# A gated recurrence on one core: decay exponents of all levels formed by VectorE, scaled inside the exponential

## The reference, cut to what matters

```
gla_log_a = log_sigmoid(glr_up) / 16
bcum  = cumsum(log_g)                        # within a chunk
decay = exp(bcum[i] - bcum[j])  for j <= i
scores[i, j] = sum_d q[i, d] k[j, d] decay[i, j, d]
o_intra = scores @ v
chunk_kv = (k * exp(b_last - bcum))^T @ v
S = exp(b_last) * S_before + chunk_kv
o_inter = (q * exp(bcum)) @ S_before
```

## Time and profile before

| what | value |
|---|---|
| time, median of 3 runs | 2365.45 us (2363.62 to 2366.69) |
| the profiled execution's own time | 2366.69 us |
| its span in the profile | 2364.9 us |
| PE busy | 2317.5 us, 98% of the span |
| DVE busy | 1290.9 us, 55% |
| ACT busy | 953.8 us, 40% |
| POOL busy | 793.8 us, 34% |
| mean granted PE clock | 0.996 of full speed |

### The profile page before, as it was taken

The page is one execution under the profiler, slowest core; times in us unless marked ns, Lnnn a source line. Parts: engine busy times, 40 slices in busy tenths (PEclk is TensorE's granted clock), DMA queues, the critical chain, the costliest instruction groups (busy, mean ns, idle before and its releaser), DMA issues.

```text
span 2364.9 us, 37976 instructions
## 1 busy us (share of the span) xinstructions
PE 2317.5 (98%) x14904; PEld 2017.3 (85%) x14904; DVE 1290.9 (55%) x2607; ACT 953.8 (40%) x1890; POOL 793.8 (34%) x707
## 2 busy tenths in 40 slices
PE   8999999999999999999999999999999999999998
PEld 7889978898888899887888898888899888888898
DVE  4003268889987433471333556456456456578746
ACT  5124665555554432332222333343343334455320
POOL 3121325555563221414442333233233242232112
PEclk9999999999999999999999999999999999999999
DMA  6234334343334421232334424324314314475621
GB/s 257 88 126 162 136 138 149 128 147 113 119 137 177 158 99 63 98 116 93 110 118 132 160 72 152 116 72 152 116 68 152 116 72 184 143 271 178 231 90 72
DMA packets 137004, 312.20 MB, mean 132 GB/s; under 512 B 12288, under 2 KB 51840, under 8 KB 125568
## 3 DMA queue, kind: packets, MB, share of 16 engines
q1 hardware_dynamic: 80192, 223.85, 27.7%
q10 hardware_dynamic: 56640, 86.00, 9.9%
HBM read 211.77 MB, written 98.04 MB: 131 GB/s over the span
## 4 chain that ended last, share of the span: by engine, by line
PE 92%; DVE 4%; DMA 1%; ACT 1%; issue 1%; POOL 0%; ACTq 0%; DVEq 0%; POOLq 0%; SPq 0%
PE bank L415 13%; PE bank L417 13%; PE bank L416 13%; PE bank L426 6%; PE bank L427 6%; PE bank L428 6%; PE bank L2702 3%; PE bank L2679 3%; PE bank L2020 3%; PE bank L2021 3%; PE bank L2022 3%; PE bank L1599 2%; PE bank L507 2%; PE bank L508 2%; PE bank L509 2%; PE bank L2668 1%
## 5 line engine op out<-in xcount | busy, mean ns | idle before, releaser
L415 PE MATMUL bank<-at_hi,w_hi 128*128 128x512 f32 x1408 | 574.1, 408 | 1.9 <-DVE stage L2213 0.9
L417 PE MATMUL bank<-at_hi,w_lo 128*128 128x512 f32 x1408 | 550.9, 391 | 0.0
L416 PE MATMUL bank<-at_lo,w_hi 128*128 128x512 f32 x1408 | 549.6, 390 | 0.0
L381 POOL TENSOR_TENSOR w_lo<-w_raw,w_hi 128x2048 fp32r<-128x2048 f32 x62 | 286.0, 4613 | 493.9 <-ACT w_hi L394 469.8
L426 PE MATMUL bank<-w_hi,at_hi 128*128 128x256 f32 x1280 | 374.1, 292 | 0.5 <-issue 0.5
L428 PE MATMUL bank<-w_hi,at_lo 128*128 128x256 f32 x1280 | 362.7, 283 | 0.0
L427 PE MATMUL bank<-w_lo,at_hi 128*128 128x256 f32 x1280 | 362.6, 283 | 0.0
L415 PEld LDWEIGHTS bank<-at_hi,w_hi 128*128 128x128 f32 x1408 | 265.6, 189 | 60.5 <-issue 8.2
L417 PEld LDWEIGHTS bank<-at_hi,w_lo 128*128 128x128 f32 x1408 | 264.5, 188 | 58.0
L304 POOL TENSOR_TENSOR small<-small,cols 128x1 f32<-128x1 f32 (+1 forms) x162 | 54.8, 338 | 757.1 <-ACT da_junk L2619 432.4
L416 PEld LDWEIGHTS bank<-at_lo,w_hi 128*128 128x128 f32 x1408 | 265.5, 189 | 48.3
(11 more groups left out here) (343 smaller groups left out, 4423.2 us busy)
## 6 DMA issues: line engine op xcount, KB each, us to landing
w_raw<-in_weights SPq DMA_DIRECT2D x84, 1024.0 KB, 7.4
feat<-stage ACTq DMA_DIRECT2D x184, 256.0 KB, 2.1
tok<-stage ACTq DMA_DIRECT2D x72, 256.0 KB, 2.2
stage<-feat SPq DMA_DIRECT2D x32, 256.0 KB, 3.5
w_mem<-in_w_mem SPq DMA_DIRECT2D x4, 1024.0 KB, 7.6
x<-in_x SPq DMA_DIRECT2D x4, 1024.0 KB, 11.4
logg<-gate_g ACTq DMA_DIRECT2D x8, 512.0 KB, 3.0
rec_b<-logg SPq DMA_DIRECT2D x16, 256.0 KB, 5.2
```

What stands on the lines that cost most here:

```text
L381: pool.tensor_tensor(w_lo[b][:], w_raw[:, b, :, :], w_hi[b][:].bitcast(F32), ALU.subtract).then_inc(w_split, 1)
L415: nc.tensor.matmul(ps_gemm[i % 2], wh, ah, start=(k == 0), stop=False)
L416: nc.tensor.matmul(ps_gemm[i % 2], wh, al, start=False, stop=False)
L417: last = nc.tensor.matmul(ps_gemm[i % 2], wl, ah, start=False, stop=(k == KT - 1))
```

## The change

- The division of the GLA log gates by 16 (L1026, four operations of 128x1024) goes; DRAM then holds undivided values. Each `Mixer` gets a scale (1/16 for GLA, 1 for HGRN), and every exponential in `decays` is taken with it.
- `exponents` no longer skips level 0: part 0 has two more operations of 128x128 and loses the negated middles (L1298). Part 1 gets one more operation of 128x256, which writes b_last − b into the KS row.
- `decays` loses the six small exponentials of a unit (L1323, L1324, L1326). Level 0 and the KS row are adjacent to the other levels in `rZ`, so each part has one exponential of 1024 columns instead of 768.

```diff
@@ -1022,8 +1022,8 @@
                     dve.wait_ge(g_act, 4 * n + h + 3)
                     if n:
                         dve.wait_ge(g_st, 32)
-                    link(dve, nc.vector.scalar_tensor_tensor(lg[h][:], lz[:, h, :], 0.0, le[h][:], ALU.min, ALU.subtract))
-                    nc.vector.tensor_scalar(lg[h][:], lg[h][:], 1.0 / TAU, None, ALU.mult).then_inc(g_dve, 1)
+                    nc.vector.scalar_tensor_tensor(lg[h][:], lz[:, h, :], 0.0, le[h][:], ALU.min,
+                                                   ALU.subtract).then_inc(g_dve, 1)
             first_dve(dve)
             dve.wait_ge(gl_ld, 48)
             with dve.Fori(0, HEADS) as it:
@@ -1077,11 +1077,11 @@
         class Mixer:
 
 
-            def __init__(self, nv, q, k, at):
-                self.nv, self.q, self.k, self.at = nv, q, k, at
-
-        gla = Mixer(2, feat1[Q1:, :], feat1[K1:, :], 0)
-        hgrn = Mixer(1, feat1[HQ - HEADS * P:, :], hgk, HEADS * P)
+            def __init__(self, nv, scale, q, k, at):
+                self.nv, self.scale, self.q, self.k, self.at = nv, scale, q, k, at
+
+        gla = Mixer(2, 1.0 / TAU, feat1[Q1:, :], feat1[K1:, :], 0)
+        hgrn = Mixer(1, 1.0, feat1[HQ - HEADS * P:, :], hgk, HEADS * P)
 
         r_banks = (ps_b[:, 1, :], ps_6)
         ps_keys, ps_kv = ps_7[:, 0:P], ps_b[:, 0, 0:2 * P]
@@ -1276,10 +1276,6 @@
         def part_levels(part):
             return range(FIRST) if part == 0 else range(FIRST, LEVELS)
 
-        def less_middle(u, c):
-
-            return small[:, 16 + 2 * u + c:17 + 2 * u + c]
-
         def ahead(head, mixer, after, n):
 
             return (head, mixer, n // 2, n % 2) if n < 2 * UNITS else (head + 1, after, n // 2 - UNITS, n % 2)
@@ -1294,17 +1290,17 @@
                 nc.vector.tensor_tensor_scan(rb[:, here], reset[:], rb[:, here], 0.0, ALU.mult, ALU.add).then_inc(r_b, 1)
                 dve.wait_ge(r_b, head * 4 + (u + 1))
                 dve.wait_ge(r_o, head * 8 + (2 * u + 2))
-                mids = rb[:, here].rearrange("p (c n) -> p c n", n=P)[:, :, BLK - 1]
-                nc.vector.tensor_scalar(small[:, 16 + 2 * u:18 + 2 * u], mids, -1.0, None, ALU.mult)
             for j in part_levels(part):
-                if j == 0:
-                    continue
                 s = P >> (j + 1)
                 d1, d2 = block_halves(rZ[:, u, j, :], s)
                 b1, b2 = block_halves(rb[:, here], s)
                 mid = b1[:, :, s - 1:s].broadcast_to([P, UNIT // (2 * s), s])
                 nc.vector.tensor_tensor(d1, mid, b1, ALU.subtract)
                 last = nc.vector.tensor_tensor(d2, b2, mid, ALU.subtract)
+            if part == 1:
+                b3 = rb[:, here].rearrange("p (c n) -> p c n", n=P)
+                last = nc.vector.tensor_tensor(rZ[:, u, KS, :].rearrange("p (c n) -> p c n", n=P),
+                                               b3[:, :, P - 1:P].broadcast_to([P, 2, P]), b3, ALU.subtract)
             last.then_inc(r_D, 1)
             if part == 1:
                 dve.wait_ge(r_in_qk[u // 2], head * 32 + 32)
@@ -1316,21 +1312,13 @@
         def decays(act, head, mixer, u, part):
             here = unit_tokens(u)
             act.wait_ge(r_D, head * 8 + (2 * u + part + 1))
-            for c in range(2):
-                b = rb[:, u * UNIT + c * P:u * UNIT + (c + 1) * P]
-                if part == 0:
-                    long = rZ[:, u, 0, c * P:(c + 1) * P]
-                    nc.scalar.activation(long[:, 0:BLK], b[:, 0:BLK], ACT.Exp, scale=-1.0, bias=b[:, BLK - 1:BLK])
-                    nc.scalar.activation(long[:, BLK:P], b[:, BLK:P], ACT.Exp, bias=less_middle(u, c))
-                else:
-                    nc.scalar.activation(rZ[:, u, KS, c * P:(c + 1) * P], b, ACT.Exp, scale=-1.0, bias=b[:, P - 1:P])
-            z = rZ[:, u, 1:FIRST, :] if part == 0 else rZ[:, u, FIRST:LEVELS, :]
-            nc.scalar.activation(z, z, ACT.Exp).then_inc(r_E, 1)
+            z = rZ[:, u, 0:FIRST, :] if part == 0 else rZ[:, u, FIRST:KS + 1, :]
+            nc.scalar.activation(z, z, ACT.Exp, scale=mixer.scale).then_inc(r_E, 1)
             if part == 0:
-                nc.scalar.activation(rZ[:, u, QS, :], rb[:, here], ACT.Exp).then_inc(r_E, 1)
+                nc.scalar.activation(rZ[:, u, QS, :], rb[:, here], ACT.Exp, scale=mixer.scale).then_inc(r_E, 1)
                 ends = rb[:, here].rearrange("p (c n) -> p c n", n=P)[:, :, P - 1]
                 act.wait_ge(r_S, head * 7 + min(2 * u + 2, 7))
-                nc.scalar.activation(rdec[:, 2 * u:2 * u + 2], ends, ACT.Exp).then_inc(r_E, 1)
+                nc.scalar.activation(rdec[:, 2 * u:2 * u + 2], ends, ACT.Exp, scale=mixer.scale).then_inc(r_E, 1)
```

## The result

The changed kernel takes 2378.99 us, median of four runs (2376.96 to 2381.91), beside 2364.53 us for the kernel before: ratio 1.0056, 95% interval 1.0041 to 1.0072. Timed once more, with other experiments, it gave 2379.37 us beside 2366.01 us (1.0056, 1.0040 to 1.0071). The forecast of 2368.8 us and its range to 2373.2 us were too low; the change costs 13.4 to 14.5 us and not 3.3.

What follows compares the result with a forecast made beforehand. PE bounds the kernel (92% of the chain), with DVE, 86% busy in the recurrence stage, having little room. 0 + 1.3 + 1.0 + 0 + 1.0 = +3.3 us on 2365.45 us gave 2368.8 us, range 2365.3 to 2373.2 us.

Steps and rivals of the forecast that it cites:

- part 2: DVE's added work in the recurrence stage: 0.65 us a unit, mostly hidden, costing 1.3 us at the start and 1.0 us in three bodies.
- the free distances: Pricing of DVE's added operations without POOL contention: 0.20 us from start to start for 128x128, 0.33 us for 128x256.
- the contention rival: Added DVE operations run in turns with POOL at start, three bodies, boundaries and tight bodies: 6.7 us, 2372.2 us; chance 0.16.
- the next tightest: Body whose `gated` ends at 610.62 us, 0.81 us before PE's product; 0.49 us left after the change, cost 0.
- Division, 0: Removing four DVE operations between 182.8 and 208.0 us, covered by a projection: 0, at most 2.8 us gain.
- Start of the stage, +1.3 us: From 330 to 353.4 us DVE is full; four parts there lengthen PE's 2.60 us stop by 1.3 us.
- Three bodies, +1.0 us: Weight-split bodies in heads 1, 3 and 5 each hold one part 1: PE's stops grow by 3 × 0.33 = 1.0 us.
- Other bodies, 0, and no fifth stop: Remaining recurrence bodies hide the added third of a microsecond; PE keeps the same four stops in L1594, cost 0.
- Boundaries, +1.0 us from −1.5 to +1.5: At head boundaries POOL's late root delays `normed`, L394, `rec_keys` and PE's state product: 0.5 us at two of three.
- The clock rival: PE's stop before 644.44 us grows to 1.86 us and triggers half clock, 1.7 us more: 2370.5 us; chance 0.17.
- ACT's relief as a gain: ACT's shorter list removes PE's boundary stops, −1.5 us, leaving +0.8 us in all: 2366.3 us; chance 0.20.
- the forecast's 3.3 us: Total for the whole kernel: division 0, start 1.3, three bodies 1.0, other bodies 0, boundaries 1.0 us, making +3.3 us.

Runs made afterwards that it cites:

- experiment 1: Kernel before plus only DVE's added operations (level 0 and KS), which ACT computes anew with its old list: 2377.72 us against 2368.51 us, ratio 1.0047.
- second profile: Profile of the unedited changed kernel, taken when it was timed once more: span 2380.4 us; that timing gave 2379.37 us, ratio 1.0056.
- Experiment 12: Changed kernel with only ACT's order at a head's end turned, evacuating and splitting before the last normed: 2376.06 us against 2368.12 us, ratio 1.0039.
- experiment 2: Kernel before without ACT's six small exponentials of a unit from head 1 on, DVE unchanged, output not the reference's: 2370.88 us, ratio 1.0014.
- experiment 3: Changed kernel with POOL's operand operations waiting until DVE has masked the chunk's scores: 2365.83 us, ratio 0.9995 against the kernel before.
- experiment 4: Kernel before with POOL's operand operations waiting until DVE has masked the chunk's scores: 2361.96 us, ratio 0.9978.
- experiment 10: Kernel before with POOL's operands held back (except head 0's first chunk) and ACT's order at a head's end turned: 2359.28 us, ratio 0.9977.
- experiment 11: Changed kernel with POOL's operands held back (except head 0's first chunk) and ACT's order at a head's end turned: 2362.36 us, ratio 0.9988.
- experiment 6: Kernel before with KS alone moved to DVE, and ACT taking levels 4 to 6 and KS in one exponential: 2370.44 us, ratio 1.0018.
- experiment 8: Changed kernel with ACT doing level 0 in four in-place operations of 64 columns again: 2378.00 us, ratio 1.0045 against the kernel before.

## Why the prediction was wrong

**The step that failed** is in part 2: "I take the free distances: POOL's list stays eight operations a unit, each delays DVE once, and the added operations stand at the end of the list." With it went the argument against the contention rival, "POOL's work is fixed". The work is fixed, its time against DVE's string isn't, for two reasons.

The first is DVE's added work itself. In experiment 1 ACT's list is the old one, and POOL's first operand operation comes as long after the root as before; yet in two bodies it gets into DVE's string, where it was held before. The first of them, POOL of the kernel before, then POOL and DVE of experiment 1:

```profile
612.43 2.96 POOL L1358 TENSOR_TENSOR rec_z<-rec_z,rec_k 128x128 f32<-128x128 f32 x1 [0.93 <-ACT rec_z L1328]
```

```profile
615.95 0.62 POOL L1360 TENSOR_TENSOR rec_z<-rec_z,rec_k 128x128 f32<-128x128 f32 x1 [0.93 <-ACT rec_z L1330]
```

```profile
616.17 0.55 DVE L1360 TENSOR_TENSOR rec_z<-rec_z,rec_k 128x128 f32<-128x128 f32 x1
```

Before, it was issued 0.53 us after the string's first operation and ended with the string. In experiment 1 it came 0.18 us after the first operation, and eight operations of DVE were slow. PE had taken the product behind this body 1.57 us after `gated` (617.51 us), and in experiment 1 it stopped before it for 1.23 us. This is not the body that I had named as the next tightest, but the one behind it.

The second is ACT's relief: POOL's operands wait for ACT's part 0, which I had made 0.78 us shorter myself, and had followed only to the boundaries. The body around 362 us shows it, POOL and ACT of the kernel before first:

```profile
361.82 3.58 POOL L306 TENSOR_TENSOR small<-small,cols 128x1 f32<-128x1 f32 x1
365.37 0.46 POOL L1358 TENSOR_TENSOR rec_z<-rec_z,rec_k 128x128 f32<-128x128 f32 x1
```

```profile
362.31 0.83 ACT L1328 ACTIVATE rec_z<-rec_z 128x768 f32<-128x768 f32 x1
```

The root's second operation begins at 361.82 us and the exponential ends at 363.14 us, 1.3 us later. This interval is 1.31 to 1.35 us in nearly every body of before. Here the root itself was held, 3.58 us. Where it takes 0.55 to 0.68 us, POOL then pauses for 0.8 to 0.9 us, and its first operand operation, issued into DVE's unbroken string, is held until the string's end: 1.9 to 3.0 us. One such body:

```profile
375.91 0.68 POOL L306 TENSOR_TENSOR small<-small,cols 128x1 f32<-128x1 f32 x1
377.36 2.04 POOL L1358 TENSOR_TENSOR rec_z<-rec_z,rec_k 128x128 f32<-128x128 f32 x1 [0.78 <-ACT rec_z L1328]
```

Either way most of POOL's eight operations run beside DVE's operations on PE's results, and DVE keeps 0.20 us; the exceptions are the three bodies with a weight split and the start. The same body in the changed kernel's first profile, POOL, ACT and DVE:

```profile
363.16 0.67 POOL L306 TENSOR_TENSOR small<-small,cols 128x1 f32<-128x1 f32 x1
363.88 0.47 POOL L1346 TENSOR_TENSOR rec_z<-rec_z,rec_k 128x128 f32<-128x128 f32 x1
364.31 0.51 POOL L1347 TENSOR_TENSOR rec_z<-rec_z,rec_q 128x128 f32<-128x128 f32 x1
```

```profile
362.69 1.05 ACT L1316 ACTIVATE rec_z<-rec_z 128x1024 f32<-128x1024 f32 x1
```

```profile
363.75 0.28 DVE L1347 TENSOR_TENSOR rec_z<-rec_z,rec_q 128x128 f32<-128x128 f32 x1
363.95 0.55 DVE L1346 TENSOR_TENSOR rec_z<-rec_z,rec_k 128x128 f32<-128x128 f32 x1
364.42 0.55 DVE L1347 TENSOR_TENSOR rec_z<-rec_z,rec_q 128x128 f32<-128x128 f32 x1
364.89 0.68 DVE L1337 TENSOR_TENSOR rec_z<-rec_z,rec_k 128x256 f32<-128x256 f32 x1
```

The exponential ends at 363.74 us, 0.58 us after the root began. POOL goes on without a pause, gets in, and the two take turns: DVE's starts lie 0.20 us apart up to 363.95 and 0.47 us from there on. Eight operations in a row are slow, 8 × 0.27 = 2.2 us for a body whose lead was 1.1 us. In the second profile the same body went the other way:

```profile
363.27 3.91 POOL L306 TENSOR_TENSOR small<-small,cols 128x1 f32<-128x1 f32 x1
367.15 0.46 POOL L1346 TENSOR_TENSOR rec_z<-rec_z,rec_k 128x128 f32<-128x128 f32 x1
```

The root was held for 3.91 us and no DVE operation was slow. All bodies in which the root ahead of the operand list is issued like this, 0.01 to 0.03 us after the first operation of DVE's string, go one of these ways. In the two profiles of the changed kernel nine such roots were let in, and eight slow operations followed each; six were held, and none followed. In the profiles of the kernel before and of experiment 1, which have the long interval, 15 were let in and 5 held, and no slow operation followed any. So the short interval turns a root that is let in into a body with turns. Which roots are let in changes between executions, which fits the wider scatter of the changed kernel; what decides it at nearly equal issue times is open.

The Trainium skill's page "SBUF — State Buffer", section "Who interferes with whom", makes issue order the judge of who blocks. The trace agrees that DVE, which issued first, holds a POOL operation back, but the hold lasts for the whole string (1.9 to 3.9 us in the rows here) and not for one operation of DVE. And where POOL issues 0.02 us behind DVE, as in the two cases above, issue order doesn't tell the outcomes apart.

**Point by point.**

- *Division, 0:* right, 0.9997 (0.9988 to 1.0006).
- *Start of the stage, +1.3 us:* the amount was right, +1.1 us, the place wasn't. The stop of 2.60 us, named to grow by 1.3 us, grew by 0.12 us; the stop before the turn at 346.41 us (1.03 us before) grew by 0.68 us, and the rest lies in the small stops ahead of it.
- *Three bodies, +1.0 us:* −0.3 us in the second profile. Two stops grew by 0.33 and 0.34 us as worked out; the one at 539 us vanished, as POOL's root was held there for 6.11 us and DVE ran free.
- *Other bodies, 0, and no fifth stop:* wrong, +5.05 us in seven new stops. This is the failed step's price in this profile. I had let the tightest body keep 0.49 us of room; a body with turns loses 2.2 us. The room was a little less than I read, too: where PE waits for `gated`, it starts 0.15 us after its end, so of the 0.81 us some 0.66 us were to spare.
- *Boundaries, +1.0 us from −1.5 to +1.5:* mechanism right, size wrong, +3.8 us. At the boundary of heads 5 and 6 in the second profile, POOL and then ACT:

```profile
671.35 3.16 POOL L304 TENSOR_TENSOR small<-small,cols 128x1 f32<-128x1 f32 x1 [3.13 <-ACT rec_junk L1476]
674.59 0.55 POOL L306 TENSOR_TENSOR small<-small,cols 128x1 f32<-128x1 f32 x1
```

```profile
675.17 0.37 ACT L1506 ACTIVATE rec_on<-bank,small 128x128 f32<-128x128 f32 x1 [2.55 <-POOL small L306]
...
676.49 1.91 ACT L394 ACTIVATE w_hi<-w_raw 128x2048 fp32r<-128x2048 f32 x1 [0.46 <-ACT stage L451]
678.31 0.26 ACT L1513 ACTIVATE rec_kT<-bank 128x128 f32<-128x128 f32 x1
```

The chain is the one named, L304, L306, `normed` (L1506), L394, `rec_keys` (L1513), and PE 2.15 us late. But the root's first operation was held for 3.16 us, against 1.82 us. I let only the string grow, by 0.33 to 0.66 us. From its first operand operation to its end it grew by 0.66 us; but the root was also issued 0.67 us earlier in the string, 0.40 us after its first operation instead of 1.07 us, since DVE has lost its lead. The two together make 1.3 us. Experiment 12, which cuts the chain, takes the stops away.
- *The rivals.* Contention was right in kind and priced at 6.7 us, half of what came: it was counted at the start, the three bodies and the boundaries, plus 0.5 us for the tight bodies. The clock rival came true beside it, in the second profile at another stop than the one named. Its stretch behind the 2.15 us stop, and the one behind the 1.87 us stop at 653.45 us:

```profile
679.50:682.80 3.30, 3.30 (x22) 2.72 (x22) 3.30 (x5) 1.72 (x4) 2.81 (x2) 0.51 0.00 0
655.00:660.00 5.00, 5.00 (x28) 4.24 (x26) 4.97 (x17) 1.90 (x6) 0.74 (x2) 1.00 0.14 46
```

1.7 us given back after the first, nothing after the second. The prediction also left out that the kernel before has such a stretch in the stage already, from 354.5 to 357.9 us behind the stop of 2.60 us; the changed kernel has it as well (355.1 to 358.5 us), so it cancels. ACT's relief as a gain did not appear; experiment 2 shows it as a loss of 0.14%.
- *The sum without POOL's list in the way:* experiments 3, 4, 10 and 11 give 3.9 and 3.1 us for the change. That the forecast's 3.3 us lies there is luck in part, for its terms do not: of 3.9 us the start has 2.4 us instead of 1.3, the boundaries 0.6 us instead of 1.0, the three bodies nothing instead of 1.0, and 0.9 us are one stop that wasn't forecast.

What is shown: most of the loss needs POOL's operands beside DVE's string (0.56% falls to 0.17%, or 3.9 us, between the two kernels with them held back); both halves and both engines' parts contribute (0.47% from DVE's additions, 0.14% from ACT's relief; 0.31% from level 0, 0.18% from KS). DVE's additions are the larger part, and ACT's relief is not needed for most of the loss. What is argued only: how the 13 to 14 us divide over held roots, turns and lost lead, since executions differ in it, and two profiles of the changed kernel and one of each other were read.

## What to carry to other kernels

When work moves from one engine to another, follow the relieved engine's signals too: whoever waits for them starts earlier, and may start into a string that it used to miss. Price such a move with the lead of every body, not of those that stop already, for an engine at 86% has little of it. Where two engines hold each other up, one wait that keeps one out of the other's string can be worth more than the operations in question: here it made the kernel before 0.22% faster and brought the changed one level with it as it was, though 3.9 us of difference between the two stay.

## What the runs showed of the hardware

- A POOL operation on one column, issued inside DVE's string of two-input operations, was held for 1.2 to 3.9 us in the rows here, and for 6.11 us in a body with a weight split; a POOL list that gets in takes turns with DVE, 0.47 us from start to start for 128x128 on DVE instead of 0.20 us. The same body of the same program went either way in two executions (0.67 us and 3.91 us for the root).
- A stop of PE of 1.87 us was followed by a granted clock of 0.50 to 0.51 (1.2 GHz) for 3.4 us in two kernels (experiments 6 and 8), and by 1.00 in the second profile of the changed one. For experiment 8, PE's row of the stop and the stretch behind it:

```profile
652.80 0.29 PE L1586 MATMUL bank<-rec_z 128*128 128x64 f32 x1 [1.87 <-DVE rec_mx L1446]
```

```profile
653.90:657.30 3.40, 3.40 (x19) 2.71 (x16) 3.37 (x13) 0.54 (x2) 0.00 (x0) 0.51 0.00 0
```

Stops of 1.87 us lie on either side, so the length of the stop alone does not decide. Experiments 3 and 4 say so more sharply: a stop of 2.29 us before 346.83 us in the one was followed by 1.00, and a stop of 1.63 us before 345.90 us in the other by 0.50 for 3.4 us.
